# A hybrid trunk kernel: the state-space layer's lag product by four column tiles, its Toeplitz tiles read from a padded store, and seven modulation groups by VectorE

## What is computed

```python
cond = silu(c)
for layer in range(2):
    mod = cond @ mod_w[layer] + mod_b[layer]           # 6 x 1024 numbers
    sh_m, sc_m, g_m, sh_f, sc_f, g_f = split(mod, 6)
    h = ada_norm(x, norm_mix_g[layer], sh_m, sc_m)
    mix = even_mixer(h, ...) if layer == 0 else s5_mixer(h, ...)
    x = x + g_m * mix
    h = ada_norm(x, norm_ffn_g[layer], sh_f, sc_f)
    ff = swiglu(h, ...) if layer == 0 else moe_swiglu(h, ...)
    x = x + g_f * ff
```

## Time and profile before

| | us |
|---|---|
| median of 3 runs | 1510.05 (1509.58 to 1510.36) |
| span of the profiled execution | 1512.1 |
| PE busy | 1430.2 (95%) |
| DVE busy | 370.1 (24%) |
| ACT busy | 159.2 (11%) |
| POOL busy | 137.5 (9%) |
| DMA | 493.91 MB, mean 327 GB/s |

### The profile page before, as it was taken

One profiled execution on the slowest core, in us unless ns is written; L12 is line 12 of the kernel. 1 busy time (PEld: TensorE's weight loads), 2 busy tenths in 40 slices (PEclk: granted clock), 3 DMA queues, 4 the chain that ended last, 5 costly groups with the idle time before them and its releaser, 6 DMA issues.

```text
span 1512.1 us, 44722 instructions
## 1 busy us (share of the span) xinstructions
PE 1430.2 (95%) x19890; PEld 1062.4 (70%) x19890; DVE 370.1 (24%) x1021; ACT 159.2 (11%) x378; POOL 137.5 (9%) x230
## 2 busy tenths in 40 slices
PE   4999999999998898999999989989989989999996
PEld 3887888888887787666567757767757755555554
DVE  2816230220203715111111111111111111113334
ACT  2103111101112203100000000000000000000001
POOL 0000043140300000000000000000000000000000
PEclk8999999999999999999999999999999999999999
DMA  9948595646328705759999999999999999999870
GB/s 385 422 165 333 194 372 216 262 188 247 140 84 356 313 0 232 326 193 426 426 421 410 426 426 395 426 426 408 427 425 407 424 427 405 413 426 394 361 308 29
DMA packets 44202, 493.91 MB, mean 327 GB/s; under 512 B 4896, under 2 KB 5152, under 8 KB 5792
## 3 DMA queue, kind: packets, MB, share of 16 engines
q1 hardware_dynamic: 41040, 475.02, 76.4%
q10 hardware_dynamic: 3024, 16.73, 2.7%
HBM read 478.10 MB, written 13.63 MB: 325 GB/s over the span
## 4 chain that ended last, share of the span: by engine, by line
PE 82%; DMA 12%; DVE 4%; ACT 1%; issue 1%; SPq 0%; POOL 0%; DVEq 0%; POOLq 0%
PE PS L744 30%; PE PS L443 20%; PE PS L753 15%; DMA ring<-in_expert_stream 9%; PE PS L598 5%; PE PS L427 2%; DMA arena<-in_expert_stream 2%; DMA ring<-in_dense_stream 2%; PE PS L762 2%; PE PS L724 1%; DVE arena L1052 1%; PE PS L652 1%; PE PS L568 1%; PE PS L580 1%; PE PS L475 1%; PE PS L417 1%
## 5 line engine op out<-in xcount | busy, mean ns | idle before, releaser
L744 PE MATMUL PS<-ring,arena 128*32 128x256 f32 x7040 | 405.4, 381 | 21.7 <-DMA ring<-in_expert_stream 13.1
L744 PEld LDWEIGHTS PS<-ring,arena 128*32 128x32 f32 x7040 | 251.5, 110 | 154.1 <-issue 16.9
L443 PE MATMUL PS<-arena,ring 128*128 128x256 f32 x1408 | 314.2, 384 | 4.3 <-ACT arena L855 2.7
L443 PEld LDWEIGHTS PS<-arena,ring 128*128 128x128 f32 x1408 | 269.9, 193 | 44.5 <-issue 6.3
L753 PE MATMUL PS<-ring,arena 128*32 128x256 f32 x4928 | 298.4, 381 | 0.8 <-DVE consts L1052 0.8
L753 PEld LDWEIGHTS PS<-ring,arena 128*32 128x32 f32 x4928 | 178.6, 111 | 91.4 <-issue 4.4
L744 PE MATMUL PS<-arena 128*32 128x256 f32 x2816 | 162.9, 382 | 10.7 <-DMA arena<-in_expert_stream 7.8
L1052 DVE TENSOR_TENSOR stat<-stat,PS 128x128 f32<-128x128 f32 x154 | 44.4, 288 | 505.3 <-ACT stat L1010 505.3
L1052 DVE TENSOR_TENSOR arena<-arena,PS 128x256 f32 (+1 forms) x123 | 55.3, 449 | 376.3 <-PE PS L443 236.5
L744 PEld LDWEIGHTS PS<-arena 128*32 128x32 f32 x2816 | 101.2, 111 | 63.9 <-DMA arena<-in_expert_stream 9.0
L1602 POOL COPY arena<-arena 128x256 f32 x153 | 61.3, 401 | 817.3 <-PE PS L744 768.8
(11 more groups left out here) (187 smaller groups left out, 603.4 us busy)
## 6 DMA issues: line engine op xcount, KB each, us to landing
ring<-in_expert_stream SPq DMA_DIRECT2D x136, 2048.0 KB, 19.9
ring<-in_dense_stream SPq DMA_DIRECT2D x105, 1024.0 KB, 7.8
arena<-in_expert_stream SPq DMA_DIRECT2D x32, 2048.0 KB, 23.2
ssm_scratch<-arena ACTq DMA_DIRECT2D x12, 1024.0 KB, 5.0
ring<-ssm_scratch SPq DMA_DIRECT2D x12, 1024.0 KB, 9.8
arena<-in_xt ACTq DMA_DIRECT2D x1, 1024.0 KB, 13.9
arena<-in_ssm_small ACTq DMA_DIRECT2D x1, 1024.0 KB, 9.1
out_t<-arena ACTq DMA_DIRECT2D x4, 256.0 KB, 2.6
```

The source lines that it names most:

```text
L443: mm = pe.matmul(PS[:, bank, j * T:(j + 1) * T], w[:, c, j * P:(j + 1) * P], moving[:, c, :], start=(c == 0), stop=(c == NC - 1))
L744: mm = pe.matmul(PS[32 * q:32 * q + 32, 0, 0:256], hbuf[:, c * BLK:(c + 1) * BLK], w[:, q * 256:(q + 1) * 256], start=(c == 0), stop=(c == ...
```

## The change

1. The lag product has its operands exchanged: `cz` (32 columns) is the weight and `bsm` (128 columns) moves, and the four tiles i of a half go to the four column tiles of the array. The result comes out turned, so step 3 turns it back by two transposes and step 4 is gone.
2. `kc` alone is spilled, 128 KB a batch, into a store `kc_scr` whose rows behind it are zeros (four transfers at the start, from zeros in the constants). The Toeplitz tiles are made by reading: eight loads of 128 KB a batch, each from another row of the store.
3. Modulation groups 12 to 18 go to VectorE. Their weights come row-wise (one output a partition, 1024 weights in it) in 14 pieces through ACT's queue into one buffer `mod_piece`; DVE multiplies with silu(c), repeated in all partitions, and sums. `ROW_PIECES` says how many pieces stand in each unit.

```diff
+ROW_MODS, GAP_MODS, ROUTER_MODS = range(12, 19), range(19, 22), range(22, MOD_GROUPS)
+ROW_PIECES = [0, 2, 2, 1, 2, 1, 2, 2, 1, 1, 0]
...
@@ side_plan
-        for s in range(5):
+        for s in range(4):
             at.setdefault(5 + 7 * q + s, []).append(("param", q, s))
...
@@ sync
             sp.wait_ge(bt_spilled, 16 * BATCHES)
-            sp.wait_ge(ct_spilled, 16 * BATCHES)
-            sp.wait_ge(t_spilled, 16 * BATCHES)
-            for n in range(SSM):
-                load(DENSE + n, ssm_scr[n])
+            for q in range(BATCHES):
+                load(DENSE + q, ssm_scr[q])
+            sp.wait_ge(kc_zeroed, 16 * BATCHES)
+            sp.wait_ge(kc_spilled, 16 * BATCHES)
+            for q in range(BATCHES):
+                n = DENSE + BATCHES + q
+                sp.wait_ge(piece_done, n - RING + 1)
+                for b in range(LB):
+                    lag = GCH * (LB - 1 - b)
+                    sp.dma_start(slot(n)[:, 256 * b:256 * (b + 1)], kc_scr[q, lag:lag + P, :]).then_inc(ring_full[n % RING], 16)
...
@@ tensor, param_step
                 if s == 2:
                     pe.wait_ge(cz_ready, q + 1)
                     bank = side_bank(use)
-                    for tile in range(BT):
+                    for half in range(2):
                         for ri in range(2):
-                            mm = pe.matmul(PS[:, bank, tile * 32:(tile + 1) * 32],
-                                           bsm[:, ri * 1024 + tile * P:ri * 1024 + (tile + 1) * P],
-                                           cz[:, ri * 256 + tile * 32:ri * 256 + (tile + 1) * 32],
-                                           start=(ri == 0), stop=(ri == 1))
+                            for i in range(4):
+                                tile = 4 * half + i
+                                mm = pe.matmul(PS[32 * i:32 * i + 32, bank, half * P:(half + 1) * P],
+                                               cz[:, ri * 256 + tile * 32:ri * 256 + (tile + 1) * 32],
+                                               bsm[:, ri * 1024 + tile * P:ri * 1024 + (tile + 1) * P],
+                                               start=(ri == 0), stop=(ri == 1), skip_group_check=True)
-                if s in (3, 4):
+                if s == 3:
                     pe.wait_ge(param_evac, USE["param", q, 2] + 1)
+                    bank = side_bank(use)
                     for half in range(2):
-                        bank = side_bank(use + half)
-                        for i in range(2):
-                            b = 4 * (s - 3) + 2 * half + i
-                            off = C_ID + GCH * (LB - 1 - b)
-                            mm = pe.matmul(PS[:, bank, i * 256:(i + 1) * 256], consts[:, off:off + P], kc,
-                                           start=True, stop=True)
-                        mm.then_inc(param_psum, 1)
+                        mm = pe.transpose(PS[:, bank, half * P:(half + 1) * P], kc_turned(q)[:, half * P:(half + 1) * P], ident)
+                    mm.then_inc(param_psum, 1)
...
@@ tensor, T product
-                w = piece().rearrange("p (g m) -> p g m", g=16)
+                w = piece().rearrange("p (b g c) -> p g b c", b=LB, g=16)
...
@@ scalar
             act.dma_start(ssm_par[:, :], ssm_in).then_inc(ssm_loaded, 16)
+            for q in range(BATCHES):
+                act.dma_start(kc_scr[q, P:P + GCH * (LB - 1), :]..., consts_in[...zeros...]).then_inc(kc_zeroed, 16)
             shift(0)
...
+                if s == 3:
+                    param_take(use, kc(q), 256)
+                    act.wait_ge(param_evac, use + 1)
+                    act.dma_start(kc_scr[q, 0:P, :], kc(q)).then_inc(kc_spilled, 16)
+
+            def row_piece(m):
+                if m:
+                    act.wait_ge(mod_piece_done, m)
+                act.dma_start(mod_piece, rows_in[m]).then_inc(mod_piece_full, 16)
...
                 act.activation(f_act, PS[:, 0, :], ACT.Silu).then_inc(gate_act, 1)
+                if f == 0:
+                    act.wait_ge(cond_row_loaded, 16)
+                    act.activation(cond_row, cond_row, ACT.Silu).then_inc(cond_row_ready, 1)
+                if ROW_PIECES[f] > 0:
+                    row_piece(sum(ROW_PIECES[:f]))
                 for n in (3 * f, 3 * f + 1, 3 * f + 2) + ((3 * FF_UNITS,) if f == FF_UNITS - 1 else ()):
                     for kind, i, s, use in PLAN.get(n, []):
+                        param_step(i, s, use)
+                if ROW_PIECES[f] > 1:
+                    row_piece(sum(ROW_PIECES[:f]) + 1)
...
@@ vector
+            def mod_dots(m):
+                dve.wait_ge(mod_piece_full, 16 * (m + 1))
+                for i in range(2):
+                    at = 4 * ROW_MODS.start + 2 * m + i
+                    d = dve.scalar_tensor_tensor(mod_piece[:, i * D:(i + 1) * D], mod_piece[:, i * D:(i + 1) * D], 1.0, cond_row,
+                                                 ALU.mult, ALU.mult, accum_out=modc[:, at:at + 1])
+                d.then_inc(mod_piece_done, 1)
...
                 if f == 0:
                     block_inputs(0)
-                for n in LATE_AT:
-                    if 3 * (f - 1) < n <= 3 * f:
-                        mod_late(LATE_AT[n])
+                if f == 1:
+                    dve.wait_ge(cond_row_ready, 1)
+                for m in range(ROW_PIECES[f]):
+                    mod_dots(sum(ROW_PIECES[:f]) + m)
                 for q in range(1, BATCHES):
```

119 lines of the change are left out of this document (49 added, 70 removed).

## The result

| | before | after |
|---|---|---|
| time, median (lowest to highest) | 1510.2 us (1509.58 to 1512.62, 4 runs) | 1484.72 us (1481.34 to 1494.16, 4 runs) |
| ratio, 95% interval | | 0.9834 [0.9811, 0.9857] |
| span of the profiled execution | 1512.1 | 1479.5 (this run's time 1481.34) |
| busy PE / DVE / POOL | 1430.2 / 370.1 / 137.5 | 1395.3 / 410.4 / 146.7 |

The kernel became faster by 1.7%, some 25 us, where 34.4 were forecast, and its runs lie further apart than those of before. Profile against profile the gain is therefore 32.6 us, and median against median 25.5.

A forecast was written before the change was run, and what follows sets the result against it. PE was taken to bound the kernel through the dense feed-forward stage. PE savings of -37.3, +2.6 for the unit 8 wait and +0.3 at the start gave -34.4 us, from 1510.05 to 1475.7 us; range 1469 to 1485.

The forecast's parts named there:

- The views: Dense stage is one unbroken line of PE; time saved there reaches the end, since the expert stream shifts with PE.
- Rival 4: Expert stream sets the end by itself, so no change: 1510 us; chance 2%.
- PE's terms: Dense stage: modulation 14.6, lag product 9.7 and Toeplitz tiles 13.0 us leave PE, 37.3 us in all.
- Start: Four stores of zeros issued on ACT ahead of shift(0): +0.3 us, between no cost and +1.3.
- Unit 8: Dots ahead of block_inputs make PE idle 3.6 us instead of 1.06: +2.6 us, bounds +2.4 and +5.2.
- Unit 4: block_inputs, queued behind unit 3's dots, ends at 32.6 us, before PE comes at 35.8: no wait.
- the ring: Load and dots sharing one buffer in the dense stage: 5.5 + 2.6 = 8 us a piece, never holding PE.
- rival 1: Slower landings and dots make block_inputs late in units 3 and 8, with a clock fall: +4 to +8 us; chance 15%.
- Clock: Old fall at 311 us probably goes (-3.4), a new one may follow unit 8's idle (+3.4): 0 together.
- T: Toeplitz reloads as small loads and the T product's strided reads cost 0; bounds for the reads 0 and +3.7 us.
- Rival 3: The 32 small T loads run one after another, 215 us late, making the kernel slower at 1691 us; chance 3%.

The follow-up runs named there:

- e6: Changed kernel with zeros stored later, block_inputs ahead of the dots, and the first expert pairs loaded in the order ring slots come free; 1477.09 us.
- e1: The changed kernel run again with no edit, for its spread and a second profile; 1486.64 us.
- e7: Kernel before plus only the lag product, transposes and padded store, zeros stored late, modulation still on PE; 1490.16 us.
- e11: Kernel before plus only the seven modulation groups on DVE, with block_inputs ahead of the dots; 1499.33 us.
- e2: Changed kernel with the four stores of zeros issued behind the first four projection copies, not ahead of shift(0); 1484.82 us.
- e9: Changed kernel with POOL's CT products left out and zeros written to that store; 1484.62 us.
- e12: Changed kernel with every row piece but the first loading only its first half, so routing changes and the expert stage grows; 1723.94 us.
- e4: Changed kernel with the piece of unit 8 moved to unit 9 and the zeros stored behind the projection copies; 1479.71 us.
- e5: Changed kernel with block_inputs ahead of the dots on DVE and the zeros stored behind the projection copies; 1475.7 us.
- e8: Kernel before plus only the seven modulation groups on DVE, the matrices as they were; 1508.36 us.
- e3: Changed kernel with the piece of unit 8 moved to unit 9; 1478.66 us.

## Why the prediction was right, and where not

**The views.** That the dense stage is one line of PE, and that what leaves it there reaches the end, held: the distance from down(10) to the end is 1041.25 us for 1041.9, and e6 shows that a start of the stream at another time wins nothing. Rival 4 is out. That the distance is the same was true within 2.3 us only (1044.2 in e1), and the sum had no term for that.

**PE's terms.** Right, and each checked apart: 26.05 forecast and 25.7 measured for the matrices (e7, with the fall), 14.6 for the modulation (16.3 measured in e11, with 1.7 of a fall). The lag product was 1.01 us in place of 0.94.

**Start.** The term of 0.3 was too small. An issue of the zeros took 0.66 to 1.06 us, and the four 3.27; my bound of 0.72 an issue was below it. Shift(0) came 1.1 us later, and against e2 the first projection 1.6 us later. At the first product of the dense stage after is 2.3 us behind before, and e1 1.1.

**Unit 8.** The mechanism was right and the size was not. Forecast 3.6 us of waiting, that is +2.6, with a new fall set against the old one; measured 4.86, that is +3.8, and a fall of 2.5. The step that failed in the wait is the landing, which cost 1.4 us: "the piece is issued some 6 us ahead and needs 5.5, and POOL is idle then". POOL was not idle, for its CT work of batch 2 ran from 358 to 376 us; and its slow dots of piece 11 made the issue of piece 12 late, 4.5 us before DVE asked for it in place of 6; but e9 shows that this decided little, since a piece issued 2.8 us earlier landed only 0.3 us earlier. What is left is the landing itself, in a stretch that was full: the DMA share of the dense stage of 0.59 is a mean, and at 355 to 375 us in after it is

```profile
355.00:375.00 20.00, 20.00 (x94) 17.61 (x93) 8.30 (x10) 0.60 (x1) 16.33 (x7) 1.00 0.86 313
```

0.86. Which transfers the piece shares the engines with was not isolated; the share, the landings of 5.9 and 8.4 us, and e12, where the same piece with half the bytes comes in time at a share of 0.57, all point that way.

**Unit 4.** "Nothing of this holds PE", and behind it that in unit 3 `block_inputs` ends at 32.6 us, before PE comes at 35.8, is the step that failed for the median. It took 5.5 us a landing and 1.28 a dot, 5.5 + 2.6 = 8 us for the ring, and these are the terms that were too small. Counted as the prediction counts, from the end of up(2) (240.2 us in after, 239.05 in e1): `block_inputs(1)` ends at 35.3 in after and at 39.0 in e1, and PE comes at 36.0. The two landings, forecast 11.0 us, took 12.0 in after and 15.3 in e1 (8.9 + 6.4); the four dots, forecast 5.1, took 6.9 and 7.2. So the dots beside POOL took some 2 of the 3.2 us of room in both profiles, and the landings the rest and more: 1.0 us in after, 4.3 in e1. PE waits 3.05 to 4.33 us with slow products behind, in e1 to e4. Without POOL's products (e9) the room is 3.0 us, and with the other order on DVE (e5) 3.4 (`block_inputs(1)` done at 269.8, PE there at 273.2). Why the landings are long stays open. With whole pieces, after and e9, in which this stage starts late (first product at 189.9 to 190.0 us), have 12.0 and 11.9 us for the two, and the four that start earlier (e1 to e4, 186.9 to 188.8) have 14.4 to 16.6; no run tests whether the start is the reason. This is rival 1 as the prediction wrote it, in both units and with a fall of the clock; I had given it 15% and it came. The row that should have decided is in rows 7: a tensor_tensor of this size took 2.12 us beside POOL. I took 1.28 because most of the stage has no POOL work, and the dots that set the wait are among those that have.

**Clock.** The old fall went, and by the profiles it goes with the old lag product: in each of the three profiles that have it (before, e8, e11) one gate product behind it is slow without an idle PE (9.78, 8.66, 8.38 us), and in the eleven with the new one every slow product of the stage stands behind a wait. A new one came, so that setting the two against each other was right in the profile of after (-3.35 and +2.5). It was wrong for the runs in which unit 4 brings a second one. The rule in the Trainium skill, "TensorE: Matmul & The Clock Gate", section "Why this matters for your kernels", that a longer idle sends the clock back to half, holds in part: falls followed waits of 2.13 us (e3), 2.25 (e6), 3.05, 4.68 and more, but none followed 2.29 (e5), 2.61 (e4) and 3.35 (e12). The length of the idle alone did not decide here.

**T.** Cost nothing, as forecast: the small loads land in 2.4 us in the median and overlap, and the T product takes 3.77 us for 3.70. Rival 3 is out. The estimate of 2.3 us a load that the prediction took from the Trainium skill, "DMA: Bandwidth & Descriptors", section "Anatomy of one DMA — SWDGE (gpsimd) path", was near the 2.4 measured, though that section is on transfers issued through GpSimd and these are SP's; that they would stand one behind another was not so. The small stores are 0.94 MB and not 0.6 (four of 128 KB and four of 112 KB), which changes nothing.

**Sum.** The terms of the forecast, and what the two profiles of the changed kernel have in their place, each against the profile of before (us; PE's own terms were checked in e7 and e11 and stand as forecast):

| term | forecast | after | e1 |
|---|---|---|---|
| ahead of the stage | +0.3 | +2.3 | +1.1 |
| PE's terms | -37.3 | -37.3 | -37.3 |
| longer wait in unit 8 | +2.6 | +3.8 | +3.6 |
| wait in unit 4 | 0 | 0 | +3.05 |
| old fall of the clock gone | 0 with the next | -3.35 | -3.35 |
| new falls | 0 | +2.5 | +3.2 |
| behind the stage | 0 | -0.7 | +2.3 |
| sum | -34.4 | -32.75 | -27.4 |
| span measured | | -32.6 | -27.3 |

In after the stage itself is within 0.5 us of the forecast, but by luck: what unit 8 costs more, with its fall, is nearly what the old fall gives back. In e1 unit 4 costs 4.7 us with its fall of 1.65, the largest part of the 7.1 us that are missing, and 2.3 more lie behind the stage. The rest of the way to the median of 1484.7 us is that the profile of before is long by 3.7 and e1 by 1.9. One run, 1494.16, no profile explains. The median stands at the upper edge of the range.

With e5's order 1475.7 us were measured and 1475.7 forecast. That is the forecast of a kernel whose order had not been chosen so, and agrees by luck in its last digit: the zeros are late there, the wait is 2.29 and no fall comes.

## What to carry to other kernels

A transfer through one single buffer has no slack, so a mean DMA share says little of it: read the share and the landings of the very stretch, and take the longest landing, not the median, where an engine waits behind it. On a queue that another engine waits for, put the work that it waits for ahead of the work that waits for a transfer: three lines moved were worth 6 to 9 us here, beside the 25 of the whole change. And when a profile of one execution has a margin under a microsecond, do not count on it in the others: e1 had none where after had 0.65.

## What the runs showed of the hardware

- A scalar_tensor_tensor of 128x1024 in float32 with an accumulator takes 1.22 us alone, no more than a tensor_tensor, and the accumulator's read is an instruction of its own of 0.08 us. Beside POOL's products of the same size it takes up to 3.36 us, and without them (e9) at most 1.30. The Trainium skill, "GPSIMD Engine Reference", section "Specifications", has it that the two contend when VectorE reads two inputs from SBUF, as these dots do; the traces agree. POOL pays too (rows of after, the first alone, the others beside the dots of 363 to 368 us):

```profile
360.23 1.93 POOL L1565 TENSOR_TENSOR buf_b<-arena 128x1024 f32<-128x1024 f32 x1
...
364.66 2.79 POOL L1565 TENSOR_TENSOR arena<-arena 128x1024 f32<-128x1024 f32 x1
367.41 2.91 POOL L1565 TENSOR_TENSOR buf_b<-arena 128x1024 f32<-128x1024 f32 x1
```

  They look as if they took turns: the dot that begins at 365.59 ends at 368.52, 1.1 us after POOL's product of 364.66, and POOL's next product ends at 370.32, 1.8 us after the dot. That is about the length of each alone.

- A transfer from HBM to HBM of 112 KB holds ACT's queue for 0.66 to 1.06 us at its issue (after), one to or from SBUF mostly 0.33, now and then more (1.23 at 249.41 us in after).
- A load issued 2.8 us earlier into a full stretch landed at the same time (374.17 and 374.51 us), and one of half the bytes took nearly as long in the median (6.5 and 6.8 us).
